# One moba group's probabilities turned by DMA instead of by TensorE, and four waits at other places

## What is computed

```
s_own = jnp.einsum('bhqd,bhld->bhql', q_i, k_own).astype(jnp.float32) * scale
s_own = jnp.where(k_pos[None, :] <= q_pos[:, None], s_own, NEG_INF)
p = jax.nn.softmax(jnp.concatenate([s_sel, s_own], axis=-1), axis=-1).astype(v.dtype)
out = jnp.einsum('bhqkl,bhqkld->bhqd', p_sel, v_sel) + jnp.einsum('bhql,bhld->bhqd', p_own, v_own)
```

## Time and profile before

| | |
|---|---|
| median of 3 runs | 1334.81 us (1334.45 to 1334.81) |
| the profiled execution's own time | 1334.76 us |
| its span, first to last instruction | 1332.8 us |
| PE busy | 1323.6 us, 99% |
| DVE busy | 931.3 us, 70% |
| ACT busy | 681.2 us, 51% |
| POOL busy | 259.2 us, 19% |
| granted TensorE clock | 1.000 of 2.4 GHz |
| PE in the chain that ended last | 93% |

### The profile page before, as it was taken

One profiled execution on the slowest core, in us unless ns is written; L12 is line 12 of the kernel. 1 busy time (PEld: TensorE's weight loads), 2 busy tenths in 40 slices (PEclk: granted clock), 3 DMA queues, 4 the chain that ended last, 5 costly groups with the idle time before them and its releaser, 6 DMA issues.

```text
span 1332.8 us, 15823 instructions
## 1 busy us (share of the span) xinstructions
PE 1323.6 (99%) x6140; PEld 1093.0 (82%) x6140; DVE 931.3 (70%) x1182; ACT 681.2 (51%) x952; POOL 259.2 (19%) x256
## 2 busy tenths in 40 slices
PE   9999999999999999999999999999999999999999
PEld 7888888888878888888888888888887888888887
DVE  6666678789887675665475664887999876665653
ACT  5444455554655455444455444556545545545442
POOL 0324402043110002323003240020521000023220
PEclk9999999999999999999999999999999999999999
DMA  9877665567554547767557775645665645477671
GB/s 317 253 218 222 184 232 183 190 196 247 174 176 156 189 140 253 212 216 213 189 192 219 217 228 196 200 154 186 195 221 173 205 158 190 156 227 224 214 213 63
DMA packets 192810, 266.34 MB, mean 200 GB/s; under 512 B 81616, under 2 KB 91360, under 8 KB 192736
## 3 DMA queue, kind: packets, MB, share of 16 engines
q1 hardware_dynamic: 191552, 262.10, 62.8%
q0 software_dynamic: 896, 3.16, 0.7%
q10 hardware_dynamic: 288, 0.07, 0.0%
HBM read 245.37 MB, written 1.06 MB: 185 GB/s over the span
## 4 chain that ended last, share of the span: by engine, by line
PE 93%; DVE 5%; ACT 1%; issue 0%; DMA 0%; SPq 0%; ACTq 0%; DVEq 0%
PE psum L679 24%; PE psum L706 21%; PE psum L939 20%; PE psum L687 12%; PE psum L944 10%; DVE ring_lo L1408 1%; PE psum L897 1%; PE psum L816 1%; PE psum L800 1%; DVE probs L1689 1%; PE psum L835 1%; PE psum L901 1%; DVE qk L1788 1%; PE psum L805 1%; DVE hss L1735 1%
## 5 line engine op out<-in xcount | busy, mean ns | idle before, releaser
L1408 DVE TENSOR_TENSOR ring_lo<-raw,ring_hi 128x1024 fp32r<-128x1024 f32 x459 | 592.3, 1305 | 320.3 <-ACT ring_hi L1010 318.6
L1010 ACT ACTIVATE ring_hi<-raw 128x1024 fp32r<-128x1024 f32 x463 | 481.3, 1048 | 569.0 <-PE psum L687 235.3
L679 PE MATMUL psum<-ring_hi,hT 128*128 128x512 f32 x1408 | 348.0, 389 | 1.4 <-DVE ring_hi L1848 1.4
L679 PEld LDWEIGHTS psum<-ring_hi,hT 128*128 128x128 f32 x1408 | 264.1, 188 | 56.4 <-DVE ring_hi L1848 1.6
L939 PE MATMUL psum<-ring_hi,hT 128*128 128x512 f32 x960 | 240.6, 393 | 0.0
L939 PEld LDWEIGHTS psum<-ring_hi,hT 128*128 128x128 f32 x960 | 178.1, 188 | 38.3 <-ACT ring_hi L1010 0.7
L687 PE MATMUL psum<-ring_lo,hT 128*128 128x512 f32 x704 | 188.4, 389 | 0.0
L1310 POOL COPY planes<-gate 128x1024 uint16<-128x1024 uint16 (+1 forms) x48 | 67.9, 1444 | 532.4 <-DVE gate L1482 532.4
L687 PEld LDWEIGHTS psum<-ring_lo,hT 128*128 128x128 f32 x704 | 131.9, 188 | 27.2
L944 PE MATMUL psum<-ring_lo,hT 128*128 128x512 f32 x480 | 128.6, 390 | 0.5 <-DVE ring_lo L1408 0.5
L706 PE MATMUL psum<-ring_hi,act_hi 128*128 128x512 f32 x352 | 110.4, 389 | 0.0
(11 more groups left out here) (193 smaller groups left out, 1150.5 us busy)
## 6 DMA issues: line engine op xcount, KB each, us to landing
raw<-in_w_ffn_in SPq DMA_DIRECT2D x78, 1024.0 KB, 5.3
raw<-in_w_in SPq DMA_DIRECT2D x64, 1024.0 KB, 5.3
raw<-in_w_ffn_out SPq DMA_DIRECT2D x44, 1024.0 KB, 5.0
raw<-in_w_branch SPq DMA_DIRECT2D x16, 1024.0 KB, 5.2
raw<-in_w_ffn_in SPq DMA_DIRECT2D x19, 512.0 KB, 4.9
raw<-in_w_mem_kv SPq DMA_DIRECT2D x8, 1024.0 KB, 5.1
raw<-in_w_out SPq DMA_DIRECT2D x8, 1024.0 KB, 5.0
forget<-negc_rows POOLq DMA_DIRECT2D x2, 1024.0 KB, 7.3
```

Of the source, the lines that this page charges most:

```text
L679: pe.matmul(outs[t][:, :], hT[part][:, kc, t * P:(t + 1) * P], w[0][:, kc - first, :], start=kc == 0 and part == 0, stop=False)
L1010: act.activation(unit_out(0, step, k), view, ACT.Copy).then_inc(hi_done.sem, 1)
L1408: dve.tensor_tensor(unit_out(1, step, k), view, unit_out(0, step, k).bitcast(F32), ALU.subtract)\
```

## The change

Group 2's probabilities no longer go through PE. ACT takes their planes apart, two copies of 1536 16-bit elements into `pT`, at the place where its gate comes next (`planes`). SP issues two DMA transposes of twelve blocks each, behind the load of step `y (3,1)`; they land in `kmem` and in the place of the fox keys' columns. POOL puts the halves together in six copies of 512 elements, between the fox queries' and the fox keys' turn. The values of group 2 move on PE from the first half of `kc` to the middle of the second half of `gate (3,1)`, behind the scores of group 3; the scores of group 3 wait for group 1's result in place of group 2's, and the values of group 2 also wait until DVE has read the scores of group 3 from PSUM. Besides: DVE scales the memory keys' columns (L1635) one step and a half later; POOL's copies of the fox keys wait for the share of group 3; the first gains are loaded from POOL's queue; the first weight rows are loaded from ACT's queue.

```diff
 for engine, step, slot, branch in (
-        ("DVE", _step_of("qm", None, 1), EARLY, 0),
+        ("DVE", _step_of("gate", (1, 0)), START, 0),
...
-BY_DMA, BY_PE = (0, 1), (2, 3, 4, 5)
+BY_DMA, BY_ACT_AND_DMA, BY_PE = (0, 1), 2, (3, 4, 5)
+MOBA_TURNED_BEHIND = _step_of("y", (3, 1))
...
-    (2, _step_of("gate", (3, 0)), _step_of("gate", (3, 0), 1), _step_of("y", (3, 0)), _step_of("kc")),
+    (2, _step_of("gate", (3, 0)), _step_of("gate", (3, 0), 1), None, _step_of("gate", (3, 1), 1)),
...
-    if g not in BY_DMA:
+    if g == BY_ACT_AND_DMA:
+        TASKS.setdefault(("ACT", exps, EARLY), []).append(("planes", g))
+    if g in BY_PE:
         _plan("probsT", g, turned, pe=MIDDLE if g == 5 else END, act=START if g == 5 else EARLY, dve=START if g == 5 else EARLY)
-    _plan("values", g, summed, pe=MIDDLE if g == 5 else END, act=START if g == 5 else EARLY,
+    _plan("values", g, summed, pe=MIDDLE if g in (2, 5) else END, act=START if g == 5 else EARLY,
...
+        moba_planes_out = [words.rearrange("p t c -> p (t c)")[:, 0:768].bitcast(U16) for words in (kmem[:, :, :], qkT_buf[:, FOX % 2, 1, :, :])]
...
-                for kc in range(2):
-                    sp.dma_start(raw_unit(0, 0)[:, kc:kc + 1, :], rows(kc, 1)).then_inc(first_rows[kc], 16)
+                sp.dma_start(raw_unit(0, 0)[:, 1:2, :], rows(1, 1)).then_inc(first_rows[1], 16)
...
+                    if m == MOBA_TURNED_BEHIND:
+                        sp.wait_ge(moba_planes.sem, moba_planes.at(L, 1))
+                        for h in range(2):
+                            sp.dma_start_transpose(moba_planes_out[h].rearrange("p (b s) -> p b s", s=P),
+                                                   pT_flat.bitcast(U16)[:, 1536 * h:1536 * (h + 1)]).then_inc(moba_turned.sem, 16)
...
-                        attended(L, arg)
+                        attended(L, arg - 1 if arg - 1 == BY_ACT_AND_DMA else arg)
...
+                    elif arg == BY_ACT_AND_DMA:
+                        pe.wait_ge(moba_merged.sem, moba_merged.at(L, 1))
+                        pe.wait_ge(max_ready.sem, max_ready.at(L, arg + 2))
...
+                elif stage == "planes":
+                    act.wait_ge(pv_ready.sem, pv_ready.at(L, arg))
+                    act.wait_ge(probs_ready.sem, probs_ready.at(L, arg + 1))
+                    for h in range(2):
+                        last = act.activation(pT_flat.bitcast(U16)[:, 1536 * h:1536 * (h + 1)],
+                                              halves_of(probs[:, None, :])[:, h, 0, :], ACT.Copy)
+                    last.then_inc(moba_planes.sem, 1)
...
             act.dma_start(ident, const_d[:, 0:P]).then_inc(ident_loaded, 16)
-            act.dma_start(gains[:, 0, 0:KC], gains_d[:, 0, 0:KC]).then_inc(first_gains, 16)
+            act.dma_start(first_piece(None, 0), w1i_d[0, 0:P, 0:GROUP]).then_inc(first_rows[0], 16)
...
+            pool.dma_start(gains[:, 0, 0:KC], gains_d[:, 0, 0:KC]).then_inc(first_gains, 16)
...
                 turn_rows(L, QC_ROWS, qk[:, 0], qkT_buf[:, FOX % 2, 0])
+                pool.wait_ge(moba_turned.sem, moba_turned.at(L, 32))
+                for h in range(2):
+                    blocks = moba_planes_out[h].rearrange("p (odd q s) -> p odd q s", odd=2, q=6)
+                    for b, block_of in ((0, slice(0, 2)), (1, slice(2, 6, 2)), (2, slice(3, 6, 2))):
+                        words = pT[:, b, :].bitcast(U16).rearrange("p (j odd s h) -> p h odd j s", j=2, odd=2, h=2)
+                        last = pool.tensor_copy(words[:, h], blocks[:, :, block_of, :])
+                last.then_inc(moba_merged.sem, 1)
                 pool.wait_ge(taken_dve.sem, taken_dve.at(L, release("kc")))
+                pool.wait_ge(probs_ready.sem, probs_ready.at(L, 4))
                 turn_rows(L, KC_ROWS, qk[:, 1], qkT_buf[:, FOX % 2, 1])
...
+                        elif arg - 1 == BY_ACT_AND_DMA:
+                            dve.wait_ge(moba_planes.sem, moba_planes.at(L, 1))
```

More of the change, by code:

```diff
@@ L353, in build @@
         pT_merged = tally("pT_merged", len(BY_DMA))
+        moba_planes = tally("moba_planes", 1)
+        moba_turned = tally("moba_turned", 32)
+        moba_merged = tally("moba_merged", 1)
         pT_ps = tally("pT_ps", len(BY_PE))
```

## The result

The changed kernel takes 1341.34 us (median of 5 runs, 1340.72 to 1341.98) against 1334.81 us (1334.45 to 1334.95): ratio 1.0049, interval 1.0038 to 1.0060. I had forecast 1331.9 us, with a range of 1328.0 to 1335.6, and given "slower" one chance in ten.

The account below looks back on a forecast made before the run. PE, busy 1323.6 of 1332.8 us, was taken as the bound, with a DVE chain of nearly equal length beside it. 1334.76 - 1.45 (layer 0) - 1.6 (layer 1) + 0.2 (opening) = 1331.9 us; range 1328.0 to 1335.6.

Parts of the forecast that it names:

- The new chain, from share to share: Mixer, from group 2's share to group 3's: planes, gate, rounding, DVE's work; 25.0 us, 2.6 less than layer 0's before.
- The slower rival: ACT's strided 16-bit copies take 5.8 us, PE waits at kc's second half for a rounded unit: 1337.7 us; chance 0.07.
- a wait on `ring_hi` in the second half: Sign of being wrong: PE waits on `ring_hi` at the second half of `kc`; no size given.
- no wait before group 3's values: Sign of being wrong: PE lacks the forecast wait of about 0.7 us there, which would favour the first rival.
- the first rival: PE alone counts, DVE finds its way and all of 7.0 us comes: 1327.7 us; chance 0.15.
- The opening: Kernel start: gains from POOL's queue, weight rows issued earlier beside `x`; a loss of 0.2 us, ends -0.3 and +1.0.
- Planes pair: ACT's two copies of 1536 elements taking group 2's planes apart: 2.9 us, ends 2.0 and 5.8.
- Share to share: Group 2's share to group 3's, layer 0: 25.0 us, plus 0.75 for POOL's merging copies beside DVE's two remainders at 357.
- A new stall of 0.8 before group 3's values: PE waits there for DVE, which needs 7.8 us behind the share where PE took 6.95: 0.8 us per layer.
- the rival of the full price: Collisions cost 1.65 us at the remainders and 1.65 behind the share; gain 0.1 per layer, 1334.8 us; chance 0.17.
- The scaling: DVE's scaling of the memory keys, moved behind a late weight remainder, removes PE's stall: 0.4 us per layer.
- The landing of the transposes: Layer 0: two DMA transposes of group 2 start at 343.8 and land at 353.5, late case two more us.

Follow-up runs that it names:

- the kernel rid of both losses: The changed kernel with ScalarE's planes of group 2 put behind gate (3,0) and the opening's old load queues restored: 1330.51 us, 0.9966 against the kernel before the change.

## Why the prediction was wrong

**The step that failed** is the second point of "The new chain, from share to share": "Then the gate, 1.0, and the rounding of the next unit, 1.0. Today both are done before DVE wants them." I moved the gate back and asked only when DVE would want what stands behind it. I did not ask who waits for the gate itself, and the sum has no term for it. That is PE, and the rows I had give the size: 0.57 us to spare, against 2.9 for the planes, 0.3 for their wait for the share, and 1.3 that PE comes earlier without the transposes. 2.9 + 0.3 + 1.3 - 0.6 = 3.9 us; the traces show 3.78 and 4.13 of idle time, to which 0.16 each is added. Put behind the gate, the same planes gave 9.1 us back.

**The slower rival** had the right kind of mechanism, PE held at `kc` by the planes on ACT, but at the wrong unit (the second half's rounded one) and with the wrong condition (a pair of 5.8 us, deciding from 4.4). The pair took 2.86 us and the loss came all the same. What I listed as a sign of being wrong, a wait on `ring_hi` in the second half, is not in the trace. Another sign, no wait before group 3's values, is there, but not for the reason that I gave it (the first rival): PE comes late enough by itself.

**The granted clock** "drops out", I wrote. It does in the kernel before. It came back in with the stalls of 3.78 and 4.13 us: 3.9 us in all.

**The opening** was mis-sized: +0.2, ends -0.3 and +1.0, against 2.19 us in the trace, 1.8 by undoing it and 1.5 by adding it to the kernel before. I named the risk (the rows flow beside `x`) without pricing it. The gains, which I did price at 5.2 us, would have landed at 4.96 alone.

**What held and what did not**, by the kernel rid of both losses:
- Planes pair 2.9 us: 2.86. The Trainium skill's figures (ScalarE: Activation LUTs, section "What ACT_TABLE_LOAD costs"), which had made it 2.8, agree with the row, also for 16-bit elements at a stride.
- Share to share 25.0 us and 0.75 for collisions, 25.75: 25.6. The parts are less good than the sum: DVE stood 2.22 us and not 2.6, and the collisions cost 0.64 and 0.53 us (2.99 and 2.88 us for two remainders instead of 2.35) at other places than the two remainders that I had named, which took 2.35. That the sum agrees is in part luck.
- A new stall of 0.8 before group 3's values: 0.65 and 0.38 idle, to which 0.16 each is added. Here too errors cancel: the collision was dearer than I had it, but PE reaches group 3's transposes 0.5 us behind the end of the share (366.36 against 365.82) and not at once.
- Share 3 at 1.83 once POOL waits: 1.83. But the remainders behind it lose 1.68 us, not 1.2, at the upper end of my range of 1.65. POOL's pair of copies loses as well, 3.88 us there against 2.48. So the rival of the full price was right behind the share and wrong ahead of it.
- The scaling, 0.4 per layer: 0.48 by the run alone.
- The landing of the transposes was ahead of need, as forecast, but too long by my count: 9.7 us from the end of the planes (343.8 to 353.5), and POOL goes on 7.5 us behind the first issue (343.77 to 351.26), 8.35 us in the change. That the change has 353.81 where I had 353.5 is luck, since all of layer 0 stands 1.6 us later there.

Without the opening the forecast's sum is 1331.7 us; the kernel that does what I had assumed takes 1330.5. The middle stretch of layer 0 gained 0.8 us, where I had 1.05. The rest came in layer 1, whose middle stretch gained 2.5 us (986.23 to 1037.32 before, 984.12 to 1032.74 there), where I had 1.2: share to share took 25.3 us there (999.31 to 1024.62), not 26.5, since the collisions cost 0.7 us (3.03 for two remainders) and not 1.5.

## What to carry to other kernels

When work is put ahead of an instruction on an in-order engine, list for every instruction that it pushes back all its waiters, the releases of PSUM banks above all, and subtract each one's slack in the trace of before. In a kernel that is bound by TensorE, price a new stall of several microseconds with a slow tail behind it. And when an engine has room, put the new work behind what others wait for, then look whose wait is last: here the gate ahead of its own units, the planes behind two more, and the old opening turned +0.49% into -0.51%.

## What the runs showed of the hardware that I had not expected

- PE idle for 3.78 and 4.13 us was followed by about 13 and about 8 matmuls of 512 columns at 0.43 us each instead of 0.23, at a granted clock of 0.50 in layer 0 (1.2 GHz). Stalls of 2.39 us, one in each layer, were followed by none. Matmuls without use in the gap kept the granted clock at 1.00 and saved 3.9 us.
- One 256 KB transfer issued 0.5 us earlier on ACT's queue (1.18 against 1.67) moved the landing of the input, on SP's queue beside it, by 0.7 us (5.54 against 4.83).
- A pair of POOL copies of 1024 16-bit elements cost DVE 1.65 to 1.7 us whether it met the share or four remainders: 6.30 against 4.62. Both have two inputs in SBUF. Two remainders beside the pair of group 0 lost only 0.84.
